# Laying the activation rows of a two-block transformer kernel at other offsets within 512 bytes

## The reference, cut to what matters

```python
# first stack, per layer
proj = rms_norm(h, g) @ w_in[l]                  # 1024 -> 2560, 272 tokens
h = h + mix(proj) @ w_out[l]                     # 1024 -> 1024
g, u = split(rms_norm(h, g2) @ w_gu[l])          # 1024 -> 2 x 2816
h = h + (silu(g) * u) @ w_down[l]                # 2816 -> 1024
# second stack, layer 0, on 256 + 256 tokens
y = even_mixer(modulate(x, ...)) @ w_out         # w_in_ab: 1024 -> 2560
# conv_ffn: w_up 1024 -> 2 x 2816, a convolution over 3 tokens, silu(g) * a, w_down 2816 -> 1024
# second stack, layer 1: the same on 256 tokens, with w_qkv and 16 query heads
```

## Time and profile before

| what | value |
|---|---|
| median of 3 runs | 1693.38 us (1692.57 to 1695.65) |
| the profiled execution: device time | 1691.35 us |
| its span, first to last instruction | 1689.6 us |
| TensorE busy | 1616.5 us, 96% of the span |
| weight loads / VectorE / ScalarE busy | 1407.3 / 1017.9 / 870.0 us |
| mean granted TensorE clock | 0.994 |
| DMA read from HBM | 251.09 MB, 149 GB/s over the span |

### The profile page before, as it was taken

How to read it: one execution, slowest core, us unless ns; L and a number is a source line. 1 busy time by engine, 2 the same in 40 slices (tenths; PEclk the granted TensorE clock), 3 DMA queues, 4 the chain that set the end, 5 groups by cost and what they waited for, 6 DMA issues and landing times.

```text
span 1689.6 us, 28191 instructions
## 1 busy us (share of the span) xinstructions
PE 1616.5 (96%) x11870; PEld 1407.3 (83%) x11870; DVE 1017.9 (60%) x1577; ACT 870.0 (51%) x1467; POOL 21.1 (1%) x38
## 2 busy tenths in 40 slices
PE   6999999999999999999989999999999898999997
PEld 6968999989789999987648777888888674789997
DVE  7675545465856555724555764424555777687585
ACT  6764534448545344544564543323444547766563
POOL 0000000000000000300000000000000000000000
PEclk9999999999999999999999999999999999999998
DMA  7465445354556464772202452232213530164642
GB/s 298 145 245 210 160 157 202 135 191 143 200 187 240 152 233 145 220 222 75 75 1 73 177 200 101 86 125 100 84 53 125 200 125 26 52 224 154 233 146 92
DMA packets 60524, 253.94 MB, mean 150 GB/s; under 512 B 4976, under 2 KB 8304, under 8 KB 42480
## 3 DMA queue, kind: packets, MB, share of 16 engines
q1 hardware_dynamic: 59088, 249.01, 41.6%
q0 software_dynamic: 1312, 3.15, 1.0%
HBM read 251.09 MB, written 1.05 MB: 149 GB/s over the span
## 4 chain that ended last, share of the span: by engine, by line
PE 81%; DVE 10%; ACT 6%; issue 2%; DMA 0%; SPq 0%; DVEq 0%; ACTq 0%
PE PA L917 63%; PE PA L977 3%; DVE W_t L1572 2%; PE PB L1340 2%; PE PB L852 2%; PE PA L1005 2%; ACT W_t L2299 1%; PE PB L1327 1%; PE PA L954 1%; PE PA L959 1%; PE PA L953 1%; PE PA L872 1%; PE PB L1270 1%; ACT tmp L2742 1%; PE PA L1412 1%
## 5 line engine op out<-in xcount | busy, mean ns | idle before, releaser
L917 PE MATMUL PA<-XH_t,W_t 128*128 128x256 f32 (+2 forms) x3968 | 873.3, 314 | 4.1 <-DVE W_t L1572 1.8
L917 PEld LDWEIGHTS PA<-XH_t,W_t 128*128 128x128 f32 x3968 | 650.1, 188 | 59.8 <-issue 6.0
L1572 DVE TENSOR_TENSOR W_t<-raw,W_t 128x1024 fp32r<-128x1024 f32 (+1 forms) x344 | 445.0, 1298 | 306.1 <-ACT W_t L2299 305.7
L917 PE MATMUL PA<-XL_t,W_t 128*128 128x256 f32 (+2 forms) x1984 | 620.5, 313 | 0.0
L2299 ACT ACTIVATE W_t<-raw 128x1024 fp32r<-128x1024 f32 (+1 forms) x344 | 381.4, 1113 | 155.6 <-PE PA L917 136.5
L917 PEld LDWEIGHTS PA<-XL_t,W_t 128*128 128x128 f32 x1984 | 373.1, 188 | 23.2 <-issue 0.5
L917 PE MATMUL PA<-AH_t,W_t 128*128 128x256 f32 (+2 forms) x1232 | 266.1, 311 | 0.2
L917 PEld LDWEIGHTS PA<-AH_t,W_t 128*128 128x128 f32 x1232 | 201.2, 188 | 14.1 <-DVE AL_t L1618 0.8
L917 PE MATMUL PA<-AL_t,W_t 128*128 128x256 f32 (+2 forms) x616 | 190.7, 310 | 0.0
L2457 ACT ACTIVATE tmp<-PA,par 128x512 f32<-128x512 f32 (+1 forms) x88 | 58.4, 667 | 133.0 <-PE PA L917 125.3
L1695 DVE SCALAR_TENSOR_TENSOR tmp<-PA,par,tmp 128x510 f32<-128x510 f32 (+1 forms) x88 | 53.6, 613 | 120.5 <-ACT tmp L2457 119.6
(11 more groups left out here) (275 smaller groups left out, 1576.4 us busy)
## 6 DMA issues: line engine op xcount, KB each, us to landing
raw<-in_w_ada SPq DMA_DIRECT2D x48, 1024.0 KB, 5.1
raw<-in_w_gu SPq DMA_DIRECT2D x44, 1024.0 KB, 4.8
raw<-in_w_dn SPq DMA_DIRECT2D x64, 704.0 KB, 4.0
raw<-in_w_up SPq DMA_DIRECT2D x44, 1024.0 KB, 4.8
raw<-in_w_in SPq DMA_DIRECT2D x30, 1024.0 KB, 5.5
raw<-in_w_out SPq DMA_DIRECT2D x12, 1024.0 KB, 4.8
raw<-in_w_qkv SPq DMA_DIRECT2D x6, 1024.0 KB, 6.3
raw<-in_w_outc SPq DMA_DIRECT2D x4, 1024.0 KB, 4.8
```

Source lines behind the costliest of these rows:

```text
L917: mm = pe.matmul(PA[:, (L.b0 + o) % 4, 0:T], W[:, c:c + P], X[:, k, L.x0:L.x0 + T], start=(n == 0 and m == 0 and not L.early), stop=(n == ...
L1572: dve.tensor_tensor(WL_t[:, w:w + L.cols], RAWV[:, r % RAW, part * UNIT:part * UNIT + L.cols], WHf[:, w:w + L.cols], ALU.subtract).then_in ...
```

## The change

No computation is changed. What changes is where the buffers lie.

- `A_t` takes the place of `AH_t` and `AL_t` as one tensor at the front of the memory. Its rows start at byte 128 within 512 bytes (448 before). `big` still lies under it and moves along.
- `XW_t` is one tensor for X and the weights. X rows start at byte 128 and weights at byte 136, as before.
- `SHIFT = 2`: where a stage works on 512 tokens (`T == T2`), it uses the views `XH2`, `XL2`, `AH2`, `AL2`, whose rows begin two columns later, at byte 136. That is where the blocks of weights begin, too. The writers on ScalarE and VectorE use the same views. One linear of 512 tokens keeps the old place (`kv`, the keys and values of the last layer, whose input a 256-token stage begins).
- `H_t` and `raw` move from byte 128 to byte 160 within 512. `Y`, `tmp`, `cboth` and `cphase` stay at 160.

The instructions of every engine are the same in number, kind, shape and order, and they wait for the same semaphores at the same values; only addresses differ.

```diff
+        SHIFT = 2
+        with nc.sbuf_tensor("big", [P, 2 * FH * 512], F32) as big:
+            pass
+        A_t = sb("A_t", 2 * FH * 512 + SHIFT, F32R)
+        AL_f = A_t.bitcast(F32)[:, FH * 512:2 * FH * 512]
+        AH_t, AL_t = A_t[:, 0:FH * 512], A_t[:, FH * 512:2 * FH * 512]
+        ada = sb("ada", 2 * 96)
+        small = sb("small", 56)
+        W_at = 2 * KD * 512 + SHIFT
+        XW_t = sb("XW_t", W_at + 4 * CH, F32R)
+        WH_t, WL_t = XW_t[:, W_at:W_at + 2 * CH], XW_t[:, W_at + 2 * CH:W_at + 4 * CH]
         H_t = sb("H_t", KD * TH)
-        XH_t = sb("XH_t", KD * 512, F32R)
-        XL_t = sb("XL_t", KD * 512, F32R)
         raw = sb("raw", RAW * CH)
-        W_at = 2
-        W_t = sb("W_t", W_at + 4 * CH, F32R)
...
-        AH_t = sb("AH_t", FH * 512, F32R)
-        AL_t = sb("AL_t", FH * 512, F32R)
...
+        def pair(t, at, n):
+            return (tiles(t, at, n, 512), tiles(t, at + n * 512, n, 512)), tiles(t.bitcast(F32), at, n, 512)
+
+        (XH, XL), XHf = pair(XW_t, 0, KD)
+        (XH2, XL2), XHf2 = pair(XW_t, SHIFT, KD)
...
+        (AH, AL), AHf = pair(A_t, 0, FH)
+        (AH2, AL2), AHf2 = pair(A_t, SHIFT, FH)
...
-        XV = (XH, XL)
-        ACTV = (AH, AL)
+        XV, XV2 = (XH, XL), (XH2, XL2)
+        ACTV, ACTV2 = (AH, AL), (AH2, AL2)
...
-                up = linear(kind, w_up[l], FH, T, XV, all_ready(), layer=l, tile0=FH * hf,
+                up = linear(kind, w_up[l], FH, T, XV2 if T == T2 else XV, all_ready(), layer=l, tile0=FH * hf,
...
-                    dve.tensor_tensor(AL[:, k, 0:T], prod, AHf[:, k, 0:T], ALU.subtract).then_inc(S("hid"), 1)
+                    lo, hi = (AL2, AHf2) if T == T2 else (AL, AHf)
+                    dve.tensor_tensor(lo[:, k, 0:T], prod, hi[:, k, 0:T], ALU.subtract).then_inc(S("hid"), 1)
```

More of the change, by code:

```diff
@@ L162, in program @@
         par = sb("par", NPARAM)
-        small = sb("small", 56)
-        ada = sb("ada", 2 * 96)
         mod = sb("mod", 2 * 2 * 40)
@@ L473, in ffn @@
                 down_kind = "add" if (kind == "glu" or hf == 1) else "copy"
-                dn = linear(down_kind, w_dn[l], KD, T, ACTV, lambda k, h0=up.h0: ("hid", h0 + k + 1), dst=dst, kt=FH,
+                dn = linear(down_kind, w_dn[l], KD, T, ACTV2 if T == T2 else ACTV, lambda k, h0=up.h0: ("hid", h0 + k + 1), dst=dst, kt=FH,
                             tile0=KD * hf)
@@ L536, in program @@
                 rdy = all_ready()
-                w = linear("copy", w_in2, 4, T2, XV, None, dst=prj2, held=2, ada=2,
+                w = linear("copy", w_in2, 4, T2, XV2, None, dst=prj2, held=2, ada=2,
                            parts=[(0, SEQ, tiles_ready(n, 0)), (SEQ, T2, tiles_ready(n, 1))])
@@ L559, in program @@
                 mixed = lambda k: ("a_low", 8 + k + 1)
-            w = linear("copy", w_out2 if l == 0 else w_outc, 4, T, XV, mixed, dst=YV)
+            w = linear("copy", w_out2 if l == 0 else w_outc, 4, T, XV2 if l == 0 else XV, mixed, dst=YV)
             plan.append(("linear", w))
@@ L656, in program @@
         XCH, XCL = tiles(AL_t, 0, 4, T1), tiles(AL_t, GR, 4, T1)
-        XCHf = tiles(AL_t.bitcast(F32), 0, 4, T1)
+        XCHf = tiles(AL_f, 0, 4, T1)
         RG, TT = XR, sp1(1)
@@ L725, in program @@
         m3_RL = [AL_t[:, 3584 + n * SEQ:3584 + (n + 1) * SEQ] for n in range(3)]
-        m3_RHf = [AL_t.bitcast(F32)[:, 4352 + n * SEQ:4352 + (n + 1) * SEQ] for n in range(3)]
+        m3_RHf = [AL_f[:, 4352 + n * SEQ:4352 + (n + 1) * SEQ] for n in range(3)]
         def quarters(b):
@@ L1820, in low @@
                     k, c = slice(2 * p, 2 * p + 2), slice(SEQ * v, SEQ * v + SEQ)
-                    dve.tensor_tensor(XL[:, k, c], j_xf[g % 2], XHf[:, k, c], ALU.subtract).then_inc(S("x_ready"), 1)
+                    lo, hi = (XL2, XHf2) if J.host.rhs is XV2 else (XL, XHf)
+                    dve.tensor_tensor(lo[:, k, c], j_xf[g % 2], hi[:, k, c], ALU.subtract).then_inc(S("x_ready"), 1)
                 dve.wait_ge(S("j_rc"), 3 * J.n + 1)
@@ L2175, in lowv @@
                     dve.wait_ge(S("a_hi"), P0 // 2 + v + 1)
-                    dve.tensor_tensor(XL[:, k, col:col + 256], PB[:, v % 2, 0:256],
-                                      XHf[:, k, col:col + 256], ALU.subtract).then_inc(S("a_low"), 1)
+                    lo, hi = (XL2, XHf2) if name == "a2" else (XL, XHf)
+                    dve.tensor_tensor(lo[:, k, col:col + 256], PB[:, v % 2, 0:256],
+                                      hi[:, k, col:col + 256], ALU.subtract).then_inc(S("a_low"), 1)
                 for t in range(n + 4):
@@ L2378, in hidden_high @@
                 def hidden_high(i, s, prod):
-                    act.activation(AH[:, s + i * st, 0:T], prod, ACT.Copy).then_inc(S("hid_hi"), 1)
+                    act.activation((AH2 if T == T2 else AH)[:, s + i * st, 0:T], prod, ACT.Copy).then_inc(S("hid_hi"), 1)
                 def body(i, s):
@@ L2555, in norm_act @@
                     return
+                hi = XH2 if T == T2 else XH
                 for v, (a, b, _, shift) in enumerate(n.groups):
@@ L2760, in high @@
                     act.wait_ge(S("a_o"), P0 // 2 + v + 1)
-                    act.activation(XH[:, k, col:col + 256], PB[:, v % 2, 0:256], ACT.Copy).then_inc(S("a_hi"), 1)
+                    act.activation((XH2 if name == "a2" else XH)[:, k, col:col + 256], PB[:, v % 2, 0:256], ACT.Copy).then_inc(S("a_hi"), 1)
                 for t in range(n + 4):
```

30 lines of the change are left out of this document (12 added, 18 removed).

## The result

| | before | changed |
|---|---|---|
| median of 12 runs each | 1693.6 us (1691.65 to 1698.04) | 1696.83 us (1693.01 to 1700.97) |
| span of the profiled execution | 1689.6 us | 1693.9 us |
| TensorE busy | 1616.5 us | 1620.5 us |

The ratio of the medians is 1.002, with a 95% interval of 1.001 to 1.0029. So the change costs a little where I had forecast 0.34% less time: 1696.8 us against 1687.6, inside the range (1676 to 1698), on the wrong side of no change. One of the 12 executions of the kernel of experiment 11 took 3194.74 us, nearly twice as long as its others, and is left out of that kernel's time and ratio.

What follows compares the result with a forecast made beforehand. TensorE's matmul pace was taken to bound the kernel. Terms −1.3 (A rows), −5.0 (512-token rows) and +0.5 (halves) sum to −5.8 us, from 1693.4 to 1687.6 us, range 1676 to 1698.

Steps and rivals of the forecast that it cites:

- What bounds the kernel: Whole kernel: TensorE, busy 1616.5 of 1689.6 us; in long stages time is the number of matmuls times their pace.
- A rows of 256 and 272 tokens: Down products: moving A from byte 448 to 128 gains 1.2 ns on 1056 256-token matmuls, −1.3 us; 272 tokens 0.
- Rows of 512 tokens, to byte 136: X and A rows in 512-token stages: 2.4 ns gained on each of 2064 matmuls, −5.0 us.
- the sign a choice: 512-token rows: bytes 128 and 448 both give 230.6 ns, so gain or no change; the gates spoke for gain.
- the gates: Recurrent branch: 12 matmuls of 272 columns, read as level starts, 125.0 ns each, 1 ns under X's 126.0.
- The three places of before: 256 columns: X at byte 128 115.6 ns, A at 448 116.8, X at 192 118.2; steps of 1.2 and 2.6.
- The 256-column halves: Two 512-token stages beginning with four tiles: 384 matmuls leave byte 128 for 136, 1.2 ns each, +0.5 us.
- Writers, raw, H and big: ScalarE and VectorE writing two columns later: 0; moved raw, H, big: 0, at most a few tenths of a microsecond.
- The pace stays: Rival: 512-column pace stays 230.6 ns; only A at 256 gains, halves cost: −0.8 us, 1692.6 us; chance 0.34.
- Level starts clash: Rival: 512-token rows level with weights at byte 136 lose 5.2 ns a matmul; +10.4 us, 1703.8 us; chance 0.12.
- A row that starts inside a line touches one line more: Rival: 512-column rows at byte 136 touch 129 four-column pieces, not 128, 1.8 ns more; +3.1 us, 1696.5 us; chance 0.06.
- The rule against any effect: Skill's rule for TensorE matmuls: moving rows and weights use independent ports, TensorE never waits; whole change worth 0.

Runs made afterwards that it cites:

- experiment 11: Changed kernel with 512-token X and A rows four columns ahead of the others instead of two behind; 1694.13 against kernel before's 1692.43 us, ratio 1.0009.
- experiment 1: Changed kernel without the two-column shift, every row at byte 128 within 512; 1691.09 against kernel before's 1692.57 us, ratio 0.9987.
- Experiment 6: TensorE alone, weights at columns 0, 4, 8, 12, 16, 34, rows at many starts; 512 columns: 226.7 ns at (4, 20), 233.3 at (12, 20).
- experiment 3: TensorE alone, 31 pairs (weights start, row start) in columns behind byte 128, within 256 bytes; 512 columns: (2, 0) 230.7 ns, (2, 2) 233.3, (0, 0) 226.7.
- experiment 9: Changed kernel with A, X and weights packed in one tensor, all rows and weights at 16 columns; 1696.42 us (one run), 512-column matmuls 226.9 ns.
- experiment 5: TensorE alone: narrower weight loads, other row lengths, weights at 2 with row starts 0 to 63; 512 columns: 230.8 ns at 0, 232.2 at 2, 228.9 at 3.
- experiment 10: TensorE alone, eight pairs each entered 12 or 8 times after different waits; 512 columns: (2, 12) 232.2 ns, (2, 15) 228.7 in all 12 entries.

## Why the prediction was wrong, point by point

- **What bounds the kernel: right.** TensorE's idle time didn't change, and the paces account for the result. The 512-column matmuls cost between 1.8 ns (the four pieces) and 2.0 ns (mean over all) × 2064 = +3.6 to +4.1 us, the halves some 4.1 ns × 384 = +1.6, A at 256 columns −1.2 × 1056 = −1.3: +3.9 to +4.4 us, against +4.3 in the span.
- **A rows of 256 and 272 tokens: right.** 115.6 ns as for X at the same place, −1.3 us forecast, −1.3 found (experiment 1); 272 unchanged.
- **Rows of 512 tokens, to byte 136: the step that failed, by its sign.** I took a gain of 2.4 ns, −5.0 us; it was a loss of 1.8 to 2.0 ns, about +4. The prediction called the sign a choice, and put it on the gates, which it took for rows that start level with their weights. That inference fails three times. The gates of the earlier trace rows were not level as the later runs count it: their rows are 272 columns apart in a tensor that starts at byte 448, so within 256 bytes the two rows that these 12 matmuls stream are at (16, 48) and (16, 0), 32 and 48 columns from their weights. Experiment 6 has 126.5 and 123.3 ns for these pairs at 272 columns, a mean of 124.9 where I had read 125.0. A row level with its weights at byte 136 costs 232 to 233 ns (here and in experiment 3), while one at byte 128 or 192 costs 226.7 (experiments 3 and 9): levelness is not the quantity, the pair is. And a 1 ns gain at 272 columns says nothing of 512, for the best place differs by length.
- **The three places of before.** Bytes 192 and 448 are one place, (2, 16), for they are 256 bytes apart. I took its 116.8 and 118.2 ns for the paces of two places; experiment 3 has 116.7 and 117.8 ns for it at its two turns. So the steps between places at 256 columns, by which the forecast was scaled, came from two places and not from three.
- **The 256-column halves: the right sign, mis-sized.** I charged a small step, 1.2 ns; it is 3.8 to 4.4 ns, +1.6 us instead of +0.5, inside the bound of 6.6 that I had given.
- **Writers, raw, H and big: right, 0.** No engine's time or wait shows them.
- **The rivals.** *The pace stays*: false, by 2 ns. *Level starts clash*: false as a mechanism; experiment 9 has level starts at the fastest 512-column pace of all. *A row that starts inside a line touches one line more*: it gave +3.7 on the long rows, +3.1 in all and 1696.5 us, and the result was 1696.8. The number was nearly right and the reason isn't: by it a start three columns in would cost as much, and that costs less than a start on the line (experiment 5), and the halves would cost 1.8 ns and not 4.4. I had given it 0.06; what should have raised it is that it was the only rival with a reason from the address of the row itself.
- **The rule against any effect.** By the Trainium skill ("TensorE: Matmul & The Clock Gate", Part 2, on LDWEIGHTS) a load takes nothing from the running matmul. Here the same rows with the same kind of load take 226.7 ns at (4, 20) and 233.3 at (12, 20), with nothing else running: only the start of the weights differs. The measurement decides: in this pattern the load has a part in the matmul's pace.

What stays open is the mechanism: why a pair costs what it does, and what picks one of two paces at an entry. The runs give the table and its two periods, not its cause. Whether (2, 60) has two paces when entered many times wasn't tried.

## What to carry to other kernels

Where matmuls follow one another without idle time, the start of the streamed row relative to the weights is worth up to 6% of their pace at 512 columns (226.7 to 240.0 ns) and 9% at 256 (113.3 to 123.3), it differs by row length, and it can't be argued from neighbours: measure it, with TensorE alone, for each length in use, and enter each candidate several times after waits. Where a pair kept one pace over all entries of experiment 10 and was used in a whole kernel, it had that pace there too: (2, 15) and (4, 20) at 512 columns, 228.7 and 226.7 ns against 228.7 and 226.8. One that was seen in a single sweep can't be trusted ((2, 12) and (2, 60) at 512 columns: 226.7 promised, 232 found). And look at the granted clock beside every group before comparing paces. When the sign of a term is a choice, the sum's main number should not rest on it.

## What the runs showed that I had not expected

- The pace depends on the pair of starts, with a few exceptions with a period of 64 columns (256 bytes) in their distance and of 8 columns (32 bytes) in the weights: from 226.7 to 240.0 ns at 512 columns and from 113.3 to 123.3 at 256, with 133.3 once.
- Some pairs have two paces and keep the one they entered with for a whole group: 113.3 or 118.3 ns for (4, 20) at 256 columns.
- Below 256 columns a shorter row soon stops being faster: 111.7 ns a matmul at 240, 224 and 192 columns, with the clock granted in full, in this data type and with a load for each matmul. At half the clock it is 213.3 ns for 128 and 160 columns and 213 to 214 for 192.
